# Last column tile of the down products: its second half taken as two parts of 128 tokens, each normed and stored by itself

## The reference

```python
def conv_ffn(h, conv_prev, l, p):
    u = jnp.einsum('btd,df->btf', h, p['ffn_up'][l])
    ...
    out = (val * jax.nn.silu(gate)) @ p['ffn_down'][l]
    return out, ext[:, -(CONV_W - 1):]
...
        ff, s_conv = conv_ffn(h2, conv_st[l], l, p)
        x = layer_norm(ALPHA * x + (1.0 + g2) * ff, p['ln2_w'][l], p['ln2_b'][l])
```

## Time and profile before

| | |
|---|---|
| median of 3 runs | 1140.78 us (1140.59 to 1142.77) |
| the profiled execution | 1137.38 us |
| its span, first to last instruction | 1135.5 us |
| mean granted clock of PE over it | 0.992 |
| PE busy | 1083.9 us, 95% of the span |
| DVE busy | 718.1 us, 63% |
| ACT busy | 499.1 us, 44% |
| POOL busy | 83.6 us, 7% |

### The profile page before, as it was taken

The page is one execution under the profiler, slowest core; times in us unless marked ns, Lnnn a source line. Parts: engine busy times, 40 slices in busy tenths (PEclk is TensorE's granted clock), DMA queues, the critical chain, the costliest instruction groups (busy, mean ns, idle before and its releaser), DMA issues.

```text
span 1135.5 us, 34861 instructions
## 1 busy us (share of the span) xinstructions
PE 1083.9 (95%) x15402; PEld 1014.7 (89%) x15402; DVE 718.1 (63%) x1167; ACT 499.1 (44%) x833; POOL 83.6 (7%) x144
## 2 busy tenths in 40 slices
PE   4888999999999999999999999999999999999996
PEld 2788888888888888899999999999999999999996
DVE  5457677676776766478913665867776676722236
ACT  2465364454635444353333333675454455422221
POOL 0003112030320302000000000000000000000000
PEclk9899999999999999999999999999999999999998
DMA  9612202022020302169877633143333323262221
GB/s 320 217 28 61 64 3 64 5 63 64 3 64 3 102 2 60 40 205 240 235 223 207 228 116 96 57 132 111 92 95 94 93 76 111 64 203 84 85 59 76
DMA packets 188269, 117.66 MB, mean 104 GB/s; under 512 B 6708, under 2 KB 180426, under 8 KB 187985
## 3 DMA queue, kind: packets, MB, share of 16 engines
q1 hardware_dynamic: 157301, 100.11, 29.6%
q10 hardware_dynamic: 30828, 15.42, 5.0%
HBM read 108.38 MB, written 7.31 MB: 102 GB/s over the span
## 4 chain that ended last, share of the span: by engine, by line
PE 54%; DVE 2%; DMA 0%; ACT 0%; issue 0%; DVEq 0%; ACTq 0%
PE PJ L234 34%; PE BB L234 10%; PE PJ L1697 4%; PE PJ L226 2%; PE BB L1607 1%; PE BB L226 1%; DMA AD<-in_ada_w_dram 0%; DVE XP L2328 0%; DVE XP L2325 0%; PE BB L1614 0%; PE BB L1804 0%; PE BB L1593 0%; PE BB L1690 0%; PE BB L1813 0%; ACT HR L1982 0%; PE PJ L1709 0%
## 5 line engine op out<-in xcount | busy, mean ns | idle before, releaser
L234 PE MATMUL PJ<-Hh,Wh 128*128 128x260 f32 (+1 forms) x1152 | 247.7, 296 | 3.1 <-DVE Hl L514 2.9
L234 PE MATMUL PJ<-Hl,Wh 128*128 128x260 f32 (+1 forms) x1152 | 233.6, 284 | 0.0
L234 PE MATMUL PJ<-Hh,Wl 128*128 128x260 f32 (+1 forms) x1152 | 233.1, 284 | 0.0
L234 PEld LDWEIGHTS PJ<-Hh,Wh 128*128 128x128 f32 x1152 | 177.2, 189 | 16.3 <-issue 8.1
L2131 DVE TENSOR_TENSOR Wl<-RAW,Wh 128x1024 fp32r<-128x1024 f32 (+2 forms) x101 | 117.0, 1160 | 100.8 <-ACT Wh L1865 97.6
L234 PEld LDWEIGHTS PJ<-Hh,Wl 128*128 128x128 f32 x1152 | 179.3, 189 | 0.0
L234 PEld LDWEIGHTS PJ<-Hl,Wh 128*128 128x128 f32 x1152 | 179.0, 189 | 0.0
L1865 ACT ACTIVATE Wh<-RAW 128x1024 fp32r<-128x1024 f32 (+2 forms) x101 | 101.7, 1007 | 158.6 <-PE PJ L234 131.3
L2510 DVE SCALAR_TENSOR_TENSOR ACC<-ACC,CP 128x512 f32<-128x512 f32 x88 | 66.1, 751 | 24.2 <-ACT ACC L2079 22.7
L1383 POOL TENSOR_TENSOR MO<-BP,CST 128x512 f32<-128x512 f32 x40 | 56.0, 1408 | 300.9 <-DVE KP L1246 248.8
L234 PE MATMUL BB<-Hh,Wh 128*128 128x260 f32 x352 | 71.8, 285 | 0.3 <-PEq L240 0.3
(11 more groups left out here) (427 smaller groups left out, 2140.5 us busy)
## 6 DMA issues: line engine op xcount, KB each, us to landing
RAW<-in_w_in_dram SPq DMA_DIRECT2D x46, 512.0 KB, 5.0
RAW<-in_ffn_up_dram SPq DMA_DIRECT2D x44, 512.0 KB, 3.8
AD<-in_ada_w_dram ACTq DMA_DIRECT2D x19, 512.0 KB, 5.4
RAW<-in_ffn_down_dram SPq DMA_DIRECT2D x16, 512.0 KB, 4.1
RAW<-in_ada_w_dram ACTq DMA_DIRECT2D x10, 512.0 KB, 5.6
AW<-in_ada_w_dram SPq DMA_DIRECT2D x2, 2048.0 KB, 13.9
RAW<-in_w_branch_rwkv_dram SPq DMA_DIRECT2D x8, 512.0 KB, 4.1
RAW<-in_w_out_dram SPq DMA_DIRECT2D x8, 512.0 KB, 4.1
```

What stands on the lines that cost most here:

```text
L234: mm = pe.matmul(out[:, b, 0:nb[b]], w[:, slot, kw, :], x[:, kx, c0:c0 + nb[b]], start=first and w is Wh and x is xh, stop=last and w is Wl)
```

## The change

The second half of `e` = 7 is no longer taken as 256 columns. PE first makes all 66 products for tokens 128 to 255 (row tile 1, still in `PJ[1][:, 1]`), and tells ACT by a further count of `half`; then all 66 for tokens 0 to 127 (row tile 0) into the other buffer, `PJ[0][:, 1]`. ACT gates each part by itself, PE transposes it by itself, and DVE adds, norms and finishes row tile 1 and then row tile 0, each with its own root and reciprocal. The stores go in the order 2, 3, 1, 0.

Several things change their place in PE's queue. The transposes of rows 2 and 3 stand behind six pieces of the second half where they stood behind three. The samples' first sum stands behind slots 0 and 1 of row 1's part, the second behind slot 0 of row 0's part, and the transpose of row 1 right behind the second sum.

```diff
@@ -1572,7 +1572,7 @@
                     sp.dma_start(o["conv_p"][0, 0, :, 512 * g:512 * g + n], CO[c][0:2, 0:n]).then_inc(S("st"), 16)
                     sp.dma_start(o["conv_s"][0, :, 1, 512 * g:512 * g + n], CO[c][2:2 + NS, 0:n]).then_inc(S("st"), 16)
                     g += CO_G[c]
-                for n, t in enumerate(ROWS2):
+                for n, t in enumerate((2, 3, 1, 0)):
                     if n == 3:
                         sp.wait_ge(S("sd2"), 6)
                         sp.dma_start(o["y_s"][:, 0, :], XS2[:]).then_inc(S("st"), 16)
@@ -1806,7 +1806,7 @@
 
                 def turn2(e, tiles, left):
 
-                    j = J + (e if e < KT - 1 or tiles[0] else KT)
+                    j = J + e + (2 - tiles[0] if len(tiles) == 1 else 0)
                     pe.wait_ge(S("mo1"), OUT_V + left)
                     pe.wait_ge(S("xa"), j - 1)
                     for n, t in enumerate(tiles):
@@ -1844,13 +1844,21 @@
                 mm.then_inc(S("half"), 1)
                 for q in range(3):
                     for k in range(DN_KN[q]):
-                        if q == 0 and k == 3:
+                        if q == 0 and k == 6:
                             turn2(e, (2, 3), KT)
-                        mm = khalf(pe, PJ[e % 2][:, 1, 0:256], q, k, SFh, SFl, 8 * q + k, 0, 256, q == 0 and k == 0, q == 2 and k == DN_KN[2] - 1)
+                        mm = khalf(pe, PJ[e % 2][:, 1, 0:P], q, k, SFh, SFl, 8 * q + k, P, P, q == 0 and k == 0, q == 2 and k == DN_KN[2] - 1)
+                    if q == 1:
+                        total2(0, 6)
+                mm.then_inc(S("half"), 1)
+                for q in range(3):
+                    for k in range(DN_KN[q]):
+                        if q == 1 and k == 0:
+                            turn2(e, (1,), KT + 1)
+                        mm = khalf(pe, PJ[1 - e % 2][:, 1, 0:P], q, k, SFh, SFl, 8 * q + k, 0, P, q == 0 and k == 0, q == 2 and k == DN_KN[2] - 1)
                     mm.then_inc(S("prj"), 1)
-                    if q < 2:
-                        total2(q, 6 + q)
-                turn2(e, (0, 1), KT + 1)
+                    if q == 0:
+                        total2(1, 7)
+                turn2(e, (0,), KT + 2)
                 pe.wait_ge(S("ys"), 8)
                 pe.wait_ge(S("co"), 11)
                 for k in range(KT):
@@ -2118,9 +2126,12 @@
                 gated_half(FD, e, 5, PJ[e % 2][:, 0, 0:256], 1)
                 root(2, 4, 7)
                 root_s(PJ[0][:, 0, NS:2 * NS], 8)
+                act.wait_ge(S("half"), KT + 2)
+                act.activation(FD[:, e, P:2 * P], PJ[e % 2][:, 1, 0:P], ACT.Copy, scale=MOD[:, 5 * KT + e, 0:1]).then_inc(S("mo1"), 1)
+                root(1, 2, 8)
                 act.wait_ge(S("prj"), B_DN + 3 * KT)
-                gated_half(FD, e, 5, PJ[e % 2][:, 1, 0:256], 0)
-                root(0, 2, 8)
+                act.activation(FD[:, e, 0:P], PJ[1 - e % 2][:, 1, 0:P], ACT.Copy, scale=MOD[:, 5 * KT + e, 0:1]).then_inc(S("mo1"), 1)
+                root(0, 1, 9)
                 act.wait_ge(S("t_y"), 9)
                 act.activation(XS2[:].rearrange("p (a b) -> p a b", a=2), BB[0:NS, 2:4, :], ACT.Copy).then_inc(S("sd2"), 1)
 
@@ -2542,7 +2553,7 @@
                 J = TURNS1
 
                 def add2(e, tiles):
-                    add(J + (e if e < KT - 1 or tiles[0] else KT), XP2, tiles, e, 1)
+                    add(J + e + (2 - tiles[0] if len(tiles) == 1 else 0), XP2, tiles, e, 1)
 
                 dve.wait_ge(S("uo"), FT)
                 past(dve, "ld_x", 96)
@@ -2576,17 +2587,16 @@
                 finish(x_row2, LNP2, 3)
                 s_scale(GX, 5)
                 s_affine(GX, 2).then_inc(S("ys"), 1)
-                add2(KT - 1, (0, 1))
-                dve.wait_ge(S("xa"), J + KT + 1)
-                need(mark(chunk((0, 1), 3, x_row2)))
-                joined((0, 1))
-                past(dve, "mv", 8)
-                c0 = centre(x_row2, LNP2, 0)
-                inverse(0, 2, 12)
-                need(c0)
-                finish(x_row2, LNP2, 0)
-                need(centre(x_row2, LNP2, 1))
-                finish(x_row2, LNP2, 1)
+                for n, t in enumerate((1, 0)):
+                    add2(KT - 1, (t,))
+                    dve.wait_ge(S("xa"), J + KT + 1 + n)
+                    need(mark(chunk((t,), 3, x_row2)))
+                    joined((t,))
+                    past(dve, "mv", 8 + n)
+                    ct = centre(x_row2, LNP2, t)
+                    inverse(t, t + 1, 12 + n)
+                    need(ct)
+                    finish(x_row2, LNP2, t)
 
             @block.gpsimd
             def _(pool):
```

## The result

| | before | after |
|---|---|---|
| median of 17 executions each, side by side | 1140.78 us | 1145.44 us |
| lowest and highest | 1135.54 to 1144.54 | 1142.25 to 1154.83 |
| ratio, with 95% interval | | 1.0047 [1.0027, 1.0067] |
| profiled execution, its span | 1137.38, 1135.5 | 1142.52, 1140.7 |
| second half's first product (S) | 1115.29 | 1116.70 |

The change makes the kernel slower, by 4.7 us in the medians; the interval is 3.1 to 7.6 us. The ratio is that of the means (the medians alone give 1.0041): the changed kernel's executions spread further upwards. The two profiled executions differ by 5.2 us of span, but 1.41 of it lies ahead of S, where both kernels do the same. Since S differs by some us from execution to execution, I read every tail from S on. E has grown by 3.79 us.

The account below looks back on a forecast made before the run. DVE set the end, with PE 0.5 us off; PE's new order would move the span's end from 1135.5 to 1139.50 (+4.0), 1141.4 for the profiled execution, plus 3.4 to the median scale: 1144.8 us, its own range 1143.7 to 1146.5.

Parts of the forecast that it names:

- pitch of the products: Time from one 128-column PE matmul to the next in the second half, bound by weight loads: 0.112 us, 0.119 before.
- 1. turn of rows 2 and 3: PE's transposes of these rows behind 18 matmuls, not 9: at 1117.31, delaying DVE's add by about 0.95, hidden afterwards.
- 2. first sum; centring; row 1's add: Samples' sum on PE behind 48 matmuls, not 24: 1120.89; DVE's centring at 1121.31, its add of row 1 at 1128.02.
- 3. second sum: Samples' second sum on PE, behind row 1's 66 and 24 of row 0's matmuls: starts at 1125.82.
- 4. row 1's transpose (PE stands): PE's transpose of row 1 waits for ACT's samples' root and gating until 1126.85; PE stands for 0.8 us.
- 5. row 0's products end: Row 0's last 42 matmuls on PE, after 0.15 for row 1's transpose, end at 1131.71.
- 6. row 0's add: After ACT's gating and PE's transpose, DVE adds row 0 at 1132.70; DVE was done with row 1 at 1131.57.
- 7. DVE's end; span's end: DVE takes 3.64 for row 0, to 1136.34, then 3.16 to the span's end at 1139.50: 4.0 more than 1135.5.
- DVE's 3.64 for row 0: DVE's time for one row tile by itself, add to finish: 3.64 us; the block of two tiles took 6.85 before.
- The products follow their columns: Rival: streamed columns set PE's pitch, 0.066 us, end +0.7; chance 0.13 including near cases under 0.09, 1141.4 to 1142.6.
- Like plain f32: Rival: PE's 128-column products handled like plain f32, 0.213 us each, +17.3, total 1158 us; chance 0.11.
- The clock drops: Rival: PE's granted clock falls behind row 1, costing up to 7 us more, total 1152 us; chance 0.06.

## Why the prediction was right

The forecast was 1144.8 us, the median is 1145.44; the tail was to grow by 4.0 and grew by 3.79. Step by step, all from S, since S itself was 1.41 later in this execution:

| step | predicted | measured |
|---|---|---|
| pitch of the products | 0.112 | 0.111 |
| 1. turn of rows 2 and 3 | S + 2.02 | S + 1.96 |
| 2. first sum; centring; row 1's add | S + 5.60; 6.02; 12.73 | S + 5.50; 5.97; 12.69 |
| 3. second sum | S + 10.53 | S + 10.41 |
| 4. row 1's transpose (PE stands) | S + 11.56 (0.8) | S + 11.37 (0.62 idle, 0.73 as the prediction counts) |
| 5. row 0's products end | S + 16.42 | S + 16.17 (last start 16.06, and one pitch) |
| 6. row 0's add | S + 17.41 | S + 17.16 |
| 7. DVE's end; span's end | S + 21.05; 24.21 | S + 20.92; 24.00 |

**The pitch (the price on which the sum hangs).** Right, and for the reason given: loads in the nearest rows started 0.11 apart, the kernel with half the weight columns went to 0.06, and those with 96 and 64 streamed columns stayed at 0.11 as long as the clock did. The Trainium skill (TensorE: Matmul & The Clock Gate, section Back-to-back issue gap) has some 81 ns for such a matmul with its load; no run here shows it for these products, and the measurement decides: 0.111. The same page's section LDWEIGHTS has a load take its columns divided by 1.2 GHz, which is 107 ns for 128 columns. The traces agree: 0.111.

**What is late, and where it goes.** Steps 1 to 6 hold to 0.25. The 0.95 of step 1 was hidden by the later wait for the first sum, as said. The stand behind the second sum was in the way as priced: without it E is 0.7 less. One figure of the last part didn't follow from the steps: some 1.3 of idle time ahead of the centring. By them DVE is ready at 1118.40 + 0.95 = 1119.35 and the centring starts at 1121.31, which is 1.96; measured 1.95. For the idle time ahead of row 0's add it had some 1.1, and 0.71 was measured: PE was 0.25 earlier than put, DVE's row 1 some 0.15 longer.

**DVE's 3.64 for row 0.** It was 1137.62 - 1133.86 = 3.76; a tenth more, about what the tail behind DVE was less (3.08 for 3.16). The 0.21 by which the tail grew less than forecast is thus 0.25 less on PE, 0.12 more on DVE and 0.08 less behind it; that the last two nearly cancel is luck.

**The rivals.** *The products follow their columns* is out for loads of 128 weight columns; at 64 both the stream and the load would give the 0.06. *Like plain f32* is out: products of 128 columns have 276 ns each, at the pitch of their loads. *The clock drops* is in part true. It got 0.06 as a case that lasts from row 1 on; in one of four profiles of the changed kernel it came, 13.8 us in, and cost 2.2. Among the 17 timed executions six are above 1146.8, with a mean granted clock over the whole span of 0.983 to 0.990, where the five fastest all had 0.994; none of the 17 of before was above 1144.54. A mean over the span doesn't say where the clock was low. One execution of the kernel with 256-column products and the norm by parts had 1144.18 and 0.987, and its profile shows the loss ahead of S (1121.65) with E 20.75; from 40 to 100 us its clock was 0.91 in the mean, for 0.97 in the kernel before. So it stays open how much of the 0.9 us between the medians' difference (4.7) and the tail's (3.8) is this fall; the interval of the ratio alone would cover it. The prediction has no term for this 0.9; less the 0.21 above it is the 0.6 by which the median lies over the forecast.

The row that I had set against a clock drop, a long stretch of narrow matmuls at full clock, was no proof: between the narrow ones that stretch has 1141 products of 260 and 268 columns (L234), and it isn't this load and stream alternating.

## What to carry to other kernels

In this kernel a product that loads 128 weight columns cost 0.11 us at full clock, whether it streamed 128 columns, 96 or 64, so halving the streamed tokens from 256 to 128 nearly doubled PE's time in that stretch (last product at S + 16.06 for S + 8.39), and a finer pipeline behind it must win more than the whole of that; here it won back 2.7 of 6.5. Before splitting, look who sets the end: here DVE was never free, and splitting its work only adds to it. And don't take the longest new wait for what sets the end: DVE's wait for the samples' first sum moved its queue by 2.5 us, but PE came to row 0 no earlier, so an earlier sum would have turned one wait into the other.

## What the runs showed of the hardware that I had not expected

The granted clock fell to 0.50 while PE worked without a gap, in the two kernels that stream less than 128 columns beside each load of 128: after 4.5 us of products with 64 columns and after 7.1 us with 96, each time with PE busy for all of the stretch. The pitch went from 0.11 to 0.21, so the loads took twice as long at half the clock. With 128 columns the clock held for 25.8 us in a stretch without a stand, and in two of five profiles it fell some 2.5 us behind a short stand (0.62 idle); in the three profiles of such products without this stand it held. Why it falls in some executions and not in others isn't settled, nor is whether the stand has a part in it: these are single executions. The kernel with narrow weights, which streams 128 columns at a pitch of 0.06, kept a clock of 1.00 for all of its products, the last of which starts at 1124.15; it has the same stand, but its products end 2.6 us behind it.
